# Retention's scores and values: two float32 products turned into three rounded ones each, with the low parts made by ScalarE and VectorE

## The reference, cut to what matters

```python
rq = rotary(r_q.reshape(b, s_len, RET_HEADS, RET_QK_DIM))
rk = rotary(r_k.reshape(b, s_len, RET_HEADS, RET_QK_DIM)) * (RET_QK_DIM ** -0.5)
rv = r_v.reshape(b, s_len, RET_HEADS, RET_V_DIM)
o_ret = retention(rq.transpose(0, 2, 1, 3), rk.transpose(0, 2, 1, 3), rv.transpose(0, 2, 1, 3))
o_ret = head_rmsnorm(o_ret.transpose(0, 2, 1, 3)).reshape(b, s_len, RET_V_WIDTH)
o_ret = jax.nn.silu(r_g) * o_ret
```

## Time and profile before

| | us |
|---|---|
| median of 3 runs | 2057.64 (2056.8 to 2061.68) |
| the profiled execution | 2056.03 |
| its span (first to last instruction) | 2054.3 |
| PE busy | 2013.1 (98%) |
| DVE, ACT, POOL busy | 1046.3, 944.1, 920.7 |
| retention, four heads | about 332 to 745 on the span's clock |

### The profile page before, as it was taken

One profiled execution on the slowest core, in us unless ns is written; L12 is line 12 of the kernel. 1 busy time (PEld: TensorE's weight loads), 2 busy tenths in 40 slices (PEclk: granted clock), 3 DMA queues, 4 the chain that ended last, 5 costly groups with the idle time before them and its releaser, 6 DMA issues.

```text
span 2054.3 us, 31073 instructions
## 1 busy us (share of the span) xinstructions
PE 2013.1 (98%) x11334; PEld 1672.3 (81%) x11334; DVE 1046.3 (51%) x1370; ACT 944.1 (46%) x1191; POOL 920.7 (45%) x430
## 2 busy tenths in 40 slices
PE   9999999999999999999999999988999999999999
PEld 5888878787878788899998887777898778888887
DVE  4354433454545454776664437876661266555312
ACT  4476662323323243555553247678663335444321
POOL 3232234242424244366654447768365134444453
PEclk9999999999999999999999999999999999999999
DMA  8111113333242422233333222210234023322331
GB/s 334 62 62 62 62 64 122 138 113 137 99 151 97 153 89 96 68 107 102 104 110 101 95 84 71 72 63 3 100 126 134 31 82 103 96 98 92 102 103 62
DMA packets 56105, 202.87 MB, mean 99 GB/s; under 512 B 6224, under 2 KB 8400, under 8 KB 54608
## 3 DMA queue, kind: packets, MB, share of 16 engines
q1 hardware_dynamic: 56016, 201.65, 28.9%
HBM read 199.53 MB, written 2.10 MB: 98 GB/s over the span
## 4 chain that ended last, share of the span: by engine, by line
PE 74%; issue 9%; DVE 7%; ACT 4%; POOL 4%; DMA 1%; DVEq 0%; POOLq 0%; SPq 0%; ACTq 0%
PE acc L2365 13%; PE acc L2367 12%; PE acc L2366 12%; PE aux L2365 6%; PE aux L2367 6%; PE aux L2366 6%; PE aux L2763 3%; PE aux L2765 3%; PE aux L2764 3%; POOL w_lo L577 3%; PE acc L2669 2%; POOL cfy L615 1%; DVE qkvf L2023 1%; PE aux L2567 1%; DMA ada<-in_ada 1%
## 5 line engine op out<-in xcount | busy, mean ns | idle before, releaser
L577 POOL TENSOR_TENSOR w_lo<-raw,w_hi 128x1024 fp32r<-128x1024 f32 x315 | 771.7, 2455 | 1078.2 <-ACT w_hi L649 1077.3
L649 ACT ACTIVATE w_hi<-raw 128x1024 fp32r<-128x1024 f32 x315 | 332.9, 1060 | 573.8 <-PE acc L2367 311.6
L2365 PE MATMUL acc<-x_hi,w_hi 128*128 128x512 f32 (+1 forms) x1016 | 399.5, 393 | 7.9 <-DVEq L1356 2.3
L2366 PE MATMUL acc<-x_lo,w_hi 128*128 128x512 f32 (+1 forms) x1016 | 392.8, 387 | 0.0
L2367 PE MATMUL acc<-x_hi,w_lo 128*128 128x512 f32 (+1 forms) x1016 | 392.8, 387 | 0.0
L2365 PEld LDWEIGHTS acc<-x_hi,w_hi 128*128 128x128 f32 x1016 | 191.2, 188 | 52.1 <-DVE x_lo L1641 4.8
L2367 PEld LDWEIGHTS acc<-x_hi,w_lo 128*128 128x128 f32 x1016 | 191.2, 188 | 39.5
L2366 PEld LDWEIGHTS acc<-x_lo,w_hi 128*128 128x128 f32 x1016 | 191.3, 188 | 37.4 <-issue 0.5
L1398 DVE SCALAR_TENSOR_TENSOR adac<-ada,c_act,adac 128x1024 f32<-128x1024 f32 x28 | 40.2, 1435 | 93.5 <-DMA ada<-in_ada 93.0
L615 POOL TENSOR_TENSOR cfy<-cfy,tn 128x512 f32<-128x512 f32 x51 | 70.0, 1372 | 20.7 <-ACT tn L649 17.9
L2365 PE MATMUL aux<-x_hi,w_hi 128*128 128x512 f32 x192 | 75.1, 391 | 1.3 <-POOL w_lo L577 1.3
(11 more groups left out here) (627 smaller groups left out, 4554.8 us busy)
## 6 DMA issues: line engine op xcount, KB each, us to landing
raw<-in_weights SPq DMA_DIRECT2D x322, 512.0 KB, 3.5
ada<-in_ada SPq DMA_DIRECT2D x32, 512.0 KB, 3.7
ada<-in_ada_first SPq DMA_DIRECT2D x8, 1024.0 KB, 12.2
resid<-in_x SPq DMA_DIRECT2D x2, 1024.0 KB, 6.3
out<-resid SPq DMA_DIRECT2D x16, 128.0 KB, 1.8
decay<-in_tables SPq DMA_DIRECT2D x4, 256.0 KB, 3.5
memf<-in_mem SPq DMA_DIRECT2D x1, 1024.0 KB, 4.8
angles<-in_tables SPq DMA_DIRECT2D x1, 512.0 KB, 6.3
```

What stands on the lines that cost most here:

```text
L577: nc.gpsimd.tensor_tensor(lo_home(u), raw[s][:], hi_home(u).bitcast(F32), ALU.subtract).then_inc(lo_ready, 1)
L649: return nc.scalar.activation(out, in_, func, **kw)
L2365: M(out, a_hi, b_hi, start=first, stop=False)
L2366: M(out, a_hi, b_lo, start=False, stop=False)
```

## The change

The scores and the values of retention are computed as three rounded matmuls per product, like the weight products.

- ScalarE makes `rq_hi` and `rk_hi` (128 x 1024 each) between its `split_hi` calls at the start of a head, `rv` is written rounded straight from PSUM (same four copies), and `rsc_hi` in two pieces (512 and 768 columns) behind `split_hi` of u0+12 and ahead of the second gate.
- VectorE makes `rq_lo`, `rk_lo`, four `rv_lo` (from PSUM) and two `rsc_lo`. They are put between the modulation steps: two steps, rotation of k, `rq_lo`, one step, `rk_lo`, two steps, `rv_lo`, one step, `rsc`, `rsc_lo`, one step, squares, one step, gate products. So six steps stand ahead of `rsc` where there were eight.
- TensorE waits for six low parts ahead of the scores and for two ahead of the values.
- The four `rsc` multiplications come in the order 0, 1, 3, 2.
- The new tiles lie in the memory of old ones (the low parts over their sources, the high parts of q and k over `oraw`, `rsc_hi` over `orh`, `rv_lo` over `orl`). Two semaphores are renamed.

```diff
             with loop(act, RET_H, [...]) as i:
                 u0 = At(U0["ret"], i, 16)
                 for j in range(8):
                     split_hi(u0 + j + AHEAD)
+                    if j in (3, 5):
+                        own["qk_rot"].next()
+                        own["attn_hi"].own(f(*((rq_hi[:], rq[:]) if j == 3 else (rk_hi[:], rk[:]))))
...
                 def gate(e):
                     split_hi(u0 + 8 + e + AHEAD)
+                    if e == 1:
+                        for c in RSC_PART:
+                            own["rsc_ready"].next()
+                            own["attn_hi"].own(f(rsc_hi[:, c], rsc[:, c]))
                     act.wait_ge(unit_used, (u0 + 8 + e + 1).val())
...
                 rotate(u0, rq)
                 ada_steps(2)
                 rotate(u0 + 2, rk)
-                ada_steps(KT - 2)
+                def attn_low(out, src, hi):
+                    own["attn_hi"].next()
+                    own["attn_split"].own(V.tensor_tensor(out, src, hi.bitcast(F32), ALU.subtract))
+
+                attn_low(rq_lo[:], rq[:], rq_hi[:])
+                ada_steps(1)
+                attn_low(rk_lo[:], rk[:], rk_hi[:])
+                ada_steps(2)
+                for b in range(NB):
+                    own["rv_ready"].next()
+                    own["attn_split"].own(V.tensor_tensor(rv_lo[:, b, :], aux[:, (2 + b) * T:(3 + b) * T],
+                                                          rv[:, b, :].bitcast(F32), ALU.subtract))
+                ada_steps(1)
                 own["rsc_done"].next()
...
+                for c in RSC_PART:
+                    attn_low(rsc_lo[:, c], rsc[:, c], rsc_hi[:, c])
+                ada_steps(1)
                 for e in range(RET_VT):
                     own["oraw_ready"].next()
                     square(oraw[:, e, :], e == 0, e == RET_VT - 1)
+                ada_steps(1)
...
-                own["qk_rot"].next(2)
-                own["rv_ready"].next(4)
+                own["attn_split"].next(2 + NB)
                 for j in TRI_ORDER:
                     a, w = TRI_AT[j], TRI_W[j]
                     for k in range(RET_QT):
-                        m = M(aux[:, a:a + w], rk[:, k, j * P:(j + 1) * P], rq[:, k, j * P:T],
-                              start=k == 0 and j != 3, stop=k == RET_QT - 1, skip_group_check=True)
+                        c = slice(j * P, (j + 1) * P)
+                        for n, (ks, qs) in enumerate(((rk_hi, rq_hi), (rk_hi, rq_lo), (rk_lo, rq_hi))):
+                            m = M(aux[:, a:a + w], ks[:, k, c], qs[:, k, j * P:T], start=n == k == 0 and j != 3,
+                                  stop=n == 2 and k == RET_QT - 1, skip_group_check=True)
                 m.then_inc(S["rsc_done"], 1)
                 tile(u0 + 9, t0 + 5, x_hi, x_lo)
-                own["rsc_ready"].next()
+                own["attn_split"].next(2)
...
-                        m = M(bank(t)[:, j * P:T], rv[:, j, e * P:(e + 1) * P], rsc[:, a:a + w],
-                              start=j == 0, stop=j == NB - 1)
+                        c = slice(e * P, (e + 1) * P)
+                        m = three(bank(t)[:, j * P:T], rv[:, j, c], rv_lo[:, j, c], rsc_hi[:, a:a + w], rsc_lo[:, a:a + w],
+                                  j == 0, j == NB - 1)
```

More of the change, by code:

```diff
@@ L300, in build_program @@
             ("angles", (P, 2 * T), F32), ("adac", (P, UNIT), F32), ("ada1", (P, UNIT), F32))
+        rq_lo, rk_lo = [put(n, (P, RET_QT, T), F32R, where=over + a * RET_QT * T * 4)[0] for a, n in enumerate(("rq_lo", "rk_lo"))]
+        at_oraw = over + (2 * RET_QT + NB) * T * 4 + TRI * 4
+        rq_hi, rk_hi = [put(n, (P, RET_QT, T), F32R, where=at_oraw + a * RET_QT * T * 4)[0]
+                        for a, n in enumerate(("rq_hi", "rk_hi"))]
+        rsc_lo = put("rsc_lo", (P, TRI), F32R, where=at_oraw - TRI * 4)[0]
+        rsc_hi = put("rsc_hi", (P, TRI), F32R, where=o2)[0]
+        rv_lo = put("rv_lo", (P, NB, T), F32R, where=o2 + RET_VT * T * 4)[0]
+        RSC_PART = (slice(0, T), slice(T, TRI))
         cos, sin = angles[:, 0:T], angles[:, T:2 * T]
@@ L749, in high @@
                     own["sp_ready"].next()
-                    own["sp_hi_ready"].own(f(sp_hi[h][:], sp[h][:]))
+                    own["attn_hi"].own(f(sp_hi[h][:], sp[h][:]))
                 def probability(h):
@@ L792, in _ @@
                 split_hi(At(U0["sb_out"] + n + AHEAD))
-            with loop(act, RET_H, [(own["rv_ready"], 4), (own["tile_done"], 8), (own["oraw_ready"], 4),
+            with loop(act, RET_H, [(own["rv_ready"], 4), (own["qk_rot"], 2), (own["rsc_ready"], 2), (own["attn_hi"], 4), (own["tile_done"], 8), (own["oraw_ready"], 4),
                                    (own["stat_ready"], 1), (own["root_ready"], 1), (own["gate_ready"], 4),
@@ L1473, in low @@
                 def low(h):
-                    own["sp_hi_ready"].next()
-                    own["sp_split"].own(V.tensor_tensor(sp_lo[h][:], sp[h][:], sp_hi[h][:].bitcast(F32), ALU.subtract))
+                    own["attn_hi"].next()
+                    own["attn_split"].own(V.tensor_tensor(sp_lo[h][:], sp[h][:], sp_hi[h][:].bitcast(F32), ALU.subtract))
                 own["z_ready"].next()
@@ L1541, in _ @@
             own["tile_done"].skip(PAIRS)
[L1542 to L1543 removed]
+            with loop(dve, RET_H, [(own["recip_ready"], 1), (own["rs_ready"], 1), (step, 10 + 2 + 6 + 1 + 1 + 16), (own["qk_rot"], 2), (own["attn_hi"], 4), (own["attn_split"], 8), (own["rv_ready"], 4), (own["ada_used"], 8), (own["ada1_loaded"], 16 * KT),
+                                   (own["rsc_done"], 1), (own["rsc_ready"], 2), (own["decay_free"], 1),
                                    (own["oraw_ready"], 4), (own["sq_ready"], 1), (own["root_ready"], 1),
@@ L1550, in _ @@
                 rotate(u0 + 2, rk)
-                ada_steps(KT - 2)
+                def attn_low(out, src, hi):
+                    own["attn_hi"].next()
+                    own["attn_split"].own(V.tensor_tensor(out, src, hi.bitcast(F32), ALU.subtract))
[8 more added lines that the diff above has]
+                ada_steps(1)
                 own["rsc_done"].next()
                 dve.wait_ge(S["decay_loaded"], i * 16 + 32)
-                for j in range(NB):
+                for j in TRI_ORDER:
                     a, w = TRI_AT[j], TRI_W[j]
                     ins = V.tensor_tensor(rsc[:, a:a + w], aux[:, a:a + w], decay[:, 0:w], ALU.mult)
-                    (step if j < NB - 1 else own["rsc_ready"]).own(ins)
+                    (own["rsc_ready"] if j in (0, 2) else step).own(ins)
                 V.sem_inc(S["decay_free"], 1)
                 own["decay_free"].skip()
+                for c in RSC_PART:
+                    attn_low(rsc_lo[:, c], rsc[:, c], rsc_hi[:, c])
+                ada_steps(1)
                 for e in range(RET_VT):
@@ L2554, in log_a @@
             def log_a(h):
-                own["sp_split"].next()
+                own["attn_split"].next()
                 for j in TRI_ORDER:
@@ L2646, in _ @@
             t_ret = 32 + PAIRS
-            with loop(pe, RET_H, [(own["qk_rot"], 2), (own["rv_ready"], 4), (own["rsc_ready"], 1), (own["sq_ready"], 1), (own["recip_ready"], 1),
+            with loop(pe, RET_H, [(own["attn_split"], 8), (own["sq_ready"], 1), (own["recip_ready"], 1),
                                   (own["ada_used"], 8), (own["tile_split"], 4)]) as i:
```

4 lines of the change are left out of this document (2 added, 2 removed).

## The result

| | before | after |
|---|---|---|
| median, runs | 2056.8 us (2055.36 to 2061.68, 7 runs) | 2066.03 us (2061.3 to 2069.25, 7 runs) |
| ratio, 95% interval | | 1.0039 (1.0027 to 1.0051) |
| the profiled execution, its span | 2056.03, 2054.3 | 2069.25, 2067.5 |
| granted clock over the span | 0.997 | 0.994 |

The change makes the kernel 9.2 us slower, 0.4%. The forecast of 2053.8 us was 12 us too low, and its range of 2049.5 to 2059 does not hold the result.

A forecast was written before the change was run, and what follows sets the result against it. TensorE, busy 98% of the span, was taken as the bound. 8.0 us saved at most, less 3 x 0.45 for heads 2 to 4 and 0.4 + 2.45 in head 1, gave 3.8: 2053.8 us, range 2049.5 to 2059.

The forecast's parts named there:

- What TensorE saves: Retention scores 3.76 for 4.32 us, values 7.52 for 8.64: 1.68 us a head, 8.0 in all with head 1's wait.
- rival 3: Short rounded matmuls cost 0.19 us each: 2062, chance 0.02; or 56 ns for 128 columns: 2051, chance 0.05.
- The chain up to the low parts: VectorE, GpSimd, SyncE, ScalarE from rotation to values: third step ends R + 4.7, u0+12 rounded from R + 25.3 to 26.1.
- R: Start of a head's third modulation step before the change, right behind the rotation: 361.72 in head 1, 465.04 in head 2.
- The waits at the values: TensorE waits for rsc_lo ahead of the values: 0 to 0.9 us in heads 2 to 4, 2.0 to 2.9 in head 1.
- the round of the sixth step: Last rv_lo ends R + 18.9 to 19.5, the step R + 20.2 to 20.8; only then u0+12 loads.
- The wait for `rv_lo`: TensorE ahead of the scores: 0.1 to 0.7 us in head 1, none in heads 2 to 4.
- Behind the values: Eighth step between squares and gate products moves these by 1.3 us; costed at nothing, 0.3 us of cover left.
- the reciprocal: Behind the values it ended 1.6 us before TensorE asked for it; this cover was to absorb the eighth step's 1.3 us.
- Rival 4: Late eighth step makes TensorE wait ahead of spread or projection, by a 2.4 us GpSimd split: 2058 to 2059, chance 0.08.
- Rival 2: Sixth step locked behind GpSimd's split if rv copies come over 1.5 us late; 3 us more a head: 2066, chance 0.1.

The follow-up runs named there:

- experiment 5: Changed kernel, third modulation step ahead of rq_lo, sixth ahead of rv_lo: 2059.47 us; its second kernel also has the seventh ahead of rsc, eighth behind rsc_lo: 2048.39 us.
- experiment 3: Changed kernel with the eighth modulation step between the second and third square instead of behind the fourth: 2058.42 us, ratio to before 1.0004.
- experiments 3 and 6: The latter: four unread matmuls between spread and bank wait, in the freed-chain kernel (2052.71 us for 2059.47) and the changed kernel (2061.17 us for 2066.03).

## Why the prediction was wrong, point by point

- **What TensorE saves.** Forecast 0.56 + 1.12 = 1.68 us a head, measured 0.48 + 0.95 = 1.43. The mechanism was right, and both forms of rival 3 fell. In the kernel of experiment 5 six matmuls of 512 take 1.39 us, of 384 1.06, of 128 0.62, of 256 0.76. So a set is 0.638 us and not 0.627: the 512 columns cost 0.232 and the 256 0.127, a little more than I read. That makes 3.83 us for the scores and 7.67 for the values. Worth 1 us in all.
- **The chain up to the low parts.** Right in its order and nearly so in its times. In head 2 of after R is 471.33: `rq_lo` 1.23, the third step locked behind GpSimd for 3.22 us and over at R + 4.6 (forecast 4.7), the fourth at R + 9.7, the fifth at R + 14.8, the rounding of u0+12 at R + 26.5 for a forecast of 25.3 to 26.1, `rsc_lo` 3.56 us for both parts.
- **The waits at the values.** Forecast 0.45 in each of heads 2 to 4 and 2.45 in head 1, measured 1.3, 0.9, 1.1 and 3.6. The step that was mis-sized is the round of the sixth step: the four `rv_lo` take 3.14 us, 0.79 each, where ScalarE's copies come every 0.62, so the last ends 1.3 us behind the last copy and not some 0.7, at R + 19.8. From the unit's load to its rounding it then took 4.68 us in head 2 (493.18 to 497.86) for 4.32 to 4.57. In head 1 it was 5.63 us (383.68 to 389.31), 1.1 more than the longest that I allowed; why is not shown. Worth 3.1 us in four heads. The wait for `rv_lo` was 1.1 us for 0.4.
- **Behind the values.** This is the step that failed most: with the clock that follows, 9.4 of the 16 us between the forecast's 3.8 us gained and the 12.3 us lost. The other misses (4 us at the waits, 1 at the savings, 1.5 at the clock behind head 1's wait) turn the 3.8 gained into 2.8 lost in the profiled run, which is not told from no change; experiment 3, which takes most of this step away, lies 1.6 us above the kernel before. I costed the eighth step at nothing by the reciprocal, and for the reciprocal it was true: TensorE does not wait for the spread. But the gate products that it delays feed two consumers, and I followed only one. The other is ScalarE's in-order queue, where the last gate stands behind `orh` of the third product, and this gate's bank is what the projection needs. The cover there was 0.12 us. Rival 4 named the place, with a GpSimd split that catches a gate product as a new loss in half of the heads: 2058 to 2059. The split catches the third product in every head of the kernel before too (2.50 us); it makes the cover small and is no new loss. The plain delay does the harm, in all heads: 5.1 us.
- **The granted clock.** It is in no term of the sum: 5.8 us in the profiled run, 4.3 of them at the projection, for which experiments 3 and 6 give some 2.5 to 4 us in the medians. The trace of before could not have shown it, since TensorE has no wait of over 1.08 us in retention there, and behind that one the clock held.
- **Rival 2**, the sixth step behind GpSimd's split, gave 2066, which is the measured number by chance. The sixth step took 1.28 us in all four heads. The time came another way. Its 1.5 us of delay are too few by its own times as well: from R + 19.2 to the split at R + 21.3 it is 2.1.
- **The sum by measured terms**: of the profiled 2056.0, less 6.9, plus 1.1, 6.9, 0.3, 5.1 and 5.8 for the clock gives 2068.3, where 2069.25 was measured.

## What to carry to other kernels

An operation moved into an engine's queue delays everything behind it, and each of these has its own consumers: follow all of them, the PSUM bank that is freed in passing too, and give the smallest cover, here 0.12 us beside the 1.6 that I looked at. Where a split operand is made by two engines in order, put its rounding ahead of prefetch work in the queue; two lines in another order were worth 5.4 to 6.9 us here. The conversion won clearly with the steps placed for both queues (ratio 0.9954), and by little with the chain freed and the wait filled (0.9984). And look at the granted clock behind each wait of TensorE: here half of the 1 us waits ahead of the projection brought 1.35 to 2.9 us more at the lower clock, and none of the 12 waits of 0.64 to 1.36 us ahead of the values did, so the length of a wait does not give its cost.

## What I had not expected of the hardware

- A wait of 1.03 us of TensorE, behind a stretch of short work (column sums of one column, spreads of 128), was followed by the lower clock in 14 of 28 heads, and the lower clock lasted some 3 to 6 us (seven matmuls of 512 columns slowed in head 2 of experiment 5's first kernel, 14 in head 4 of after). Four unread matmuls in the wait kept the clock at 1.00 in eight heads of eight. Waits of 2.8 us gave both outcomes, those of 3.35 us and more (six heads) all had the fall behind them.
- VectorE and GpSimd compete for their ports within a tenth of a microsecond: the same instruction took 2.92 or 0.69 us as GpSimd began 0.01 us ahead or 0.10 us behind. Through the chain of transfers that became 3.65 us on TensorE. The Trainium skill, page "SBUF — State Buffer", section "Who interferes with whom", says that whoever issues first keeps the ports, and these rows agree.
- Behind a run of 384 columns the first of six rounded matmuls of 128 columns is followed at 0.06 us, the others at 0.11, so 0.103 on average. TensorE in the fastest kernel:

```profile
486.64 0.33 PE L2692 MATMUL aux<-rq_hi,rk_lo 128*128 128x384 f32 x1
486.81 0.22 PE L2692 MATMUL aux<-rq_hi,rk_hi 128*128 128x128 f32 x1
486.87 0.27 PE L2692 MATMUL aux<-rq_lo,rk_hi 128*128 128x128 f32 x1
486.98 0.27 PE L2692 MATMUL aux<-rq_hi,rk_lo 128*128 128x128 f32 x1
```
